# ScalarE evictions, early masks and a split FFN input in a one-core decoder step: what the change does to the time

## The reference: what is computed

```python
h = rms_norm(x, norm_mix_g); z = h @ w_in          # 512 q | 256 kv | 64 k_rope | 1024 u | 1024 v
q = rms_norm(z_q) @ w_q_up                         # 8 heads x (128 + 64 rope)
kv_c = rms_norm(z_kv); k_pe = rope(z_pe)           # latent attention
u = gelu(z_u); v = rms_norm(gelu(z_v))
cm = u * (tril(w_spatial) @ v + b)                 # in chunks of 128 positions
x += concat(rms_norm(attn), rms_norm(cm)) @ w_out
x += memory_attend(rms_norm(x)) @ w_mem_o          # 4 heads of 128, 256 memory tokens
x += square(relu(rms_norm(x) @ w_ffn_up)) @ w_ffn_down     # 8192 wide
```

## Time and profile before

| what | value |
|---|---|
| time, median of 3 runs | 2558.09 us (2555.03 to 2559.18) |
| time of the profiled execution | 2557.49 us |
| its span, first to last instruction | 2555.6 us |
| PE busy | 2417.3 us (95%) |
| DVE, ACT, POOL busy | 895.9, 630.6, 957.3 us (35%, 25%, 37%) |
| mean granted TensorE clock | 0.979 |

### The profile page before, as it was taken

One profiled execution on the slowest core, in us unless ns is written; L12 is line 12 of the kernel. 1 busy time (PEld: TensorE's weight loads), 2 busy tenths in 40 slices (PEclk: granted clock), 3 DMA queues, 4 the chain that ended last, 5 costly groups with the idle time before them and its releaser, 6 DMA issues.

```text
span 2555.6 us, 47459 instructions
## 1 busy us (share of the span) xinstructions
PE 2417.3 (95%) x18906; PEld 2353.2 (92%) x18906; DVE 895.9 (35%) x1257; ACT 630.6 (25%) x888; POOL 957.3 (37%) x412
## 2 busy tenths in 40 slices
PE   7999868688999989999999999999999999999996
PEld 7999858556899878999999999999999999999996
DVE  6200297576533567211211211211211311311366
ACT  5211352254211433211211211211211211211210
POOL 3433352232344323443433434334343343433442
PEclk9999989799999999999999999999999999999998
DMA  6665574375422242222222222222222222222222
GB/s 257 191 187 182 179 245 134 140 299 212 153 88 84 79 170 74 86 87 90 82 90 87 85 90 82 90 87 86 90 82 90 87 86 90 82 90 87 85 90 86
DMA packets 101733, 304.37 MB, mean 119 GB/s; under 512 B 12369, under 2 KB 45170, under 8 KB 96562
## 3 DMA queue, kind: packets, MB, share of 16 engines
q1 hardware_dynamic: 98784, 291.01, 32.9%
q10 hardware_dynamic: 2898, 12.66, 1.3%
HBM read 297.30 MB, written 44.08 MB: 134 GB/s over the span
## 4 chain that ended last, share of the span: by engine, by line
PE 66%; issue 18%; POOL 8%; DVE 7%; ACT 0%; POOLq 0%; DVEq 0%; ACTq 0%
PE psum L1295 63%; POOL hl L387 8%; DVE square L1148 1%; PE psum L1484 1%; DVE square_sum L1150 1%; DVE head_max L1064 1%; PE psum L1446 0%; DVE x L1145 0%; DVE x L1284 0%; DVE probs_t L1103 0%; DVE square L863 0%; DVE probs L1085 0%; DVE head_bias L1066 0%; DVE psum L1059 0%; DVE rstd_x L818 0%
## 5 line engine op out<-in xcount | busy, mean ns | idle before, releaser
L387 POOL TENSOR_TENSOR hl<-raw,hl 128x1024 fp32r<-128x1024 f32 x376 | 917.2, 2440 | 1470.9 <-ACT hl L769 926.2
L1295 PE MATMUL psum<-xg,hl 128*128 128x272 f32 x10272 | 1306.0, 289 | 28.7 <-DVE xg L813 16.7
L1295 PEld LDWEIGHTS psum<-xg,hl 128*128 128x128 f32 x10272 | 1301.4, 189 | 32.3 <-POOL hl L387 16.2
L1295 PE MATMUL psum<-ffn_hidden,hl 128*128 128x272 f32 x6144 | 772.7, 288 | 0.0
L1295 PEld LDWEIGHTS psum<-ffn_hidden,hl 128*128 128x128 f32 x6144 | 771.9, 188 | 0.0
L769 ACT CAST hl<-raw 128x1024 fp32r<-128x1024 f32 x254 | 267.2, 1052 | 1222.8 <-PE psum L1295 1222.8
L1272 DVE TENSOR_TENSOR x<-x,psum 128x544 f32 x112 | 80.8, 721 | 567.2 <-PE psum L1295 567.2
L1257 DVE SCALAR_TENSOR_TENSOR square<-psum,rstd_x 128x544 f32<-128x544 f32 x64 | 46.4, 725 | 496.7 <-PE psum L1295 496.7
L1261 DVE TENSOR_SCALAR ffn_hidden<-square 128x544 f32 x64 | 132.1, 2064 | 60.7 <-ACT square L778 60.7
L448 ACT CAST hl<-raw 128x1024 fp32r<-128x1024 f32 x64 | 67.3, 1051 | 317.7 <-PE psum L1295 317.6
L441 ACT CAST hl<-raw 128x1024 fp32r<-128x1024 f32 x58 | 60.5, 1046 | 183.2 <-PE psum L1295 124.2
(11 more groups left out here) (231 smaller groups left out, 1137.9 us busy)
## 6 DMA issues: line engine op xcount, KB each, us to landing
raw<-in_w_stream SPq DMA_DIRECT2D x376, 512.0 KB, 3.2
page_cols_gathered<-in_pool_t SPq DMA_DIRECT2D x128, 160.0 KB, 2.9
page_cols<-page_cols_gathered SPq DMA_DIRECT2D x16, 1280.0 KB, 7.1
page_rows_gathered<-in_pool_n SPq DMA_DIRECT2D x128, 128.0 KB, 2.9
page_rows<-page_rows_gathered SPq DMA_DIRECT2D x16, 1024.0 KB, 6.2
x<-in_x_t SPq DMA_DIRECT2D x8, 544.0 KB, 9.2
out<-x SPq DMA_DIRECT2D x8, 544.0 KB, 2.7
cache_k_sb<-in_mem_k_t SPq DMA_DIRECT2D x2, 2048.0 KB, 9.7
```

The costliest lines, as they stand in the source:

```text
L387: nc.gpsimd.tensor_tensor(HL[s % 2][:, 1, :, :], RAW[:, s % 4, :, :], HL[s % 2][:, 0, :, :].bitcast(F32), ALU.subtract).then_inc(w_lo, 1)
L1295: last = mm(PSUM[:, s + half, 0:HALF], HL[slot][:, wp, blk, :], src[:, xp, k, HALF * half:HALF * (half + 1)], start=start and n == 0, stop ...
```

## The change

It has five parts.

1. **Region moved.** TB goes up from 72224 to 72288 bytes, and the memory output's operand `OMH` from TB to TB + 121344.
2. **Masks early.** The 16 small multiplications that mask the spatial weights go from DVE's program just ahead of the memory values' eviction to ahead of the evictions of the input projection.
3. **Evictions on ACT.** Every second eviction of the v transposes, and all evictions of q_up and KV, go from DVE to ACT, between the `hi` of the units. DVE then has the four ropes in one piece, the sample group's rope copies, head 0's rope operands and the eight scalings of the mix result.
4. **Head 0's splits early.** ACT's three casts for head 0 stand behind the first half of KV, and POOL's three subtractions ahead of `lo(72)`; the DMA of `w_uv_sb` goes behind `hi(73)`.
5. **FFN input in MEMO.** Per tile DVE adds to x and then makes the lo part of the tile before; ACT makes the hi part and the square (two buffers); POOL adds the squares up. PE's sum of squares goes from ahead of FFN tile 0 to behind it.

The core of the diff:

```diff
-        TB = at_end[0]
+        TB = (at_end[0] + 31) // 128 * 128 + 96
...
-        OMH = place("mem_out_split", [P, 2, MH, TOK], F32R, TB)
+        OMH = place("mem_out_split", [P, 2, MH, TOK], F32R, TB + 121344)
...
             stage_qk_lo(0)
             stage_v_lo(0)
+            for n in range(U_OUT, U_OUT + 2):
+                lo(n, n + 1)
...
+            def add_square(k):
+
+                pool.wait_ge(x3_sq, k + 1)
+                if k == 0:
+                    last = nc.gpsimd.tensor_copy(ACC[:, :], TMP[0][:, :])
+                else:
+                    pool.wait_ge(x3_add, k)
+                    last = nc.gpsimd.tensor_tensor(ACC[:, :], ACC[:, :], TMP[k % 2][:, :], ALU.add)
+                last.then_inc(x3_add if k < KD - 1 else sum_ok, 1)
+
+            for i in range(8):
+                add_square(2 * i)
+                lo(U_MEMO + 2 + i, U_MEMO + 2 + i + 1)
+                add_square(2 * i + 1)
...
             hi(62)
             hi(63)
+            for n in range(1, 8, 2):
+                act.wait_ge(tr, n + 1)
+                nc.scalar.copy(VT[:, n // 2, 512:1024], PSUM[:, 4 + n % 4, :]).then_inc(tr_out_a, 1)
...
+            q_out(0)
+            act.wait_ge(mix_out, 9)
+            for k in range(4):
+                square("c", k, Z[:, Z_U + k, :])
+            hi(64)
+            q_out(1)
+            for k in range(4, 8):
+                square("c", k, Z[:, Z_U + k, :])
+            q_out(2)
+            hi(65)
+            q_out(3)
+            sqrt("c", RX, 6, 1024, TOK, [(kv_n, 2)])
+            for m in range(2, 6):
+                q_out(2 * m)
+                hi(64 + m)
+                q_out(2 * m + 1)
...
-                    act.wait_ge(t_out, G_KV + 16)
+                    act.wait_ge(t_out, G_KV + 8)
...
-            for j in range(2, 12):
-                q_out(j)
-                if j == 5:
-                    invert("c", RX)
-                if j in (6, 7, 9, 10):
...
+            invert("c", RX)
+            for r in range(4):
+                dve.wait_ge(t_out, G_QUP + r + 1)
+                if r:
+                    dve.wait_ge(q_ready, r)
+                rope(Q[:, 8 + r, :]).then_inc(q_ready, 1)
...
+            def x3_tile(k):
+                act.wait_ge(t_out, G_MEMO + k + 1)
+                nc.scalar.activation(XG[:, 0, k, :], X[:, k, :], ACT.Copy,
+                                     scale=G[:, GAINS["x3"] + k:GAINS["x3"] + k + 1]).then_inc(xg_hi, 1)
+                if k > 1:
+                    act.wait_ge(x3_add, k - 1)
+                nc.scalar.activation(TMP[k % 2][:, :], X[:, k, :], ACT.Square).then_inc(x3_sq, 1)
+
+            for i in range(8):
+                x3_tile(2 * i)
+                hi(U_MEMO + 2 + i)
+                x3_tile(2 * i + 1)
             sqrt("x3", RX, 6, D, TOK, [(t_out, G_MEMQ + 4)])
...
+            for k in range(KD):
+                if k % 2:
+                    dve.wait_ge(w_used, U_MEMO + k // 2 + 1)
+                else:
+                    dve.wait_ge(half_used, 7 + k // 2)
+                tt(two(X[:, k, :]), two(X[:, k, :]), banks(G_MEMO + k), ALU.add).then_inc(t_out, 1)
+                if k:
+                    x3_lo(k - 1)
+            x3_lo(KD - 1)
             invert("x3", RX)
...
+            ffn_up_tile(0, 0, 0)
+            sum_squares("x3", 6)
+            ffn_up_tile(0, 0, 1)
```

More of the change, by code:

```diff
@@ L388, in lo @@
                                         HL[s % 2][:, 0, :, :].bitcast(F32), ALU.subtract).then_inc(w_lo, 1)
-            with pool.Fori(0, U_OUT // 4) as i:
+            with pool.Fori(0, U_KV // 4) as i:
                 for s in range(4):
                     lo(s, i * 4 + (s + 1))
-            for n in range(U_OUT, U_OUT + 2):
+            for n in range(U_KV, U_OUT):
                 lo(n, n + 1)
@@ L603, in stage_v_hi @@
                 nc.scalar.copy(VH[:, 0, :, :], VV[:, :, 128 * h:128 * h + 128]).then_inc(v_hi, 1)
+            act.wait_ge(st_mk, 32)
+            q_out(0)
[14 more added lines that the diff above has]
+                q_out(2 * m + 1)
+            act.wait_ge(st_out, 48)
+            for h in range(4):
+                k_out(h, G_KV + h)
+            hi(70)
+            for kb in range(4):
+                v_out(kb, 0, G_KV + 4 + kb)
+            hi(71)
             stage_qk_hi(0)
             stage_v_hi(0)
+            for h in range(4, 8):
+                k_out(h, G_KV + 4 + h)
+            hi(72)
+            for kb in range(4):
+                v_out(kb, 1, G_KV + 12 + kb)
+            hi(73)
+            act.wait_ge(qabs_out, 2)
+            act.dma_start(WUV[:, :, :], w_uv_p).then_inc(ld_uv, 16)
             act.wait_ge(c_n, 8)
@@ L846, in _ @@
                     z_out(4)
+            dve.wait_ge(ld_c, 16)
+            dve.wait_ge(ld_sp, 48)
+            for g in range(8):
+                tt(WT[:, g, :], WT[:, g, :], C[:, C_TRIL:C_TRIL + 128], ALU.mult)
+                last = tt(W4[:, g, :], W4[:, g, :], C[0:NS, C_BLOCK:C_BLOCK + NS], ALU.mult)
+            last.then_inc(mask_ok, 1)
             with dve.Fori(0, 9) as i:
@@ L1008, in _ @@
             step(last)
-            dve.wait_ge(t_out, G_KV + 16)
             def stage_rope(h):
@@ L1031, in _ @@
             stage_rope(0)
+            for k in range(8):
+                g = GAINS["c"] + k
+                stt(Z[:, Z_U + k, :], Z[:, Z_U + k, :], G[:, g:g + 1], RX[:, :], ALU.mult, ALU.mult).then_inc(c_n, 1)
+            dve.wait_ge(t_out, G_KV)
             nc.vector.memset(QR[:, :, :], 0.0)
@@ L1407, in _ @@
             pe.wait_ge(mask_ok, 1)
-            pe.wait_ge(tr_out, 11)
+            pe.wait_ge(tr_out, 6)
+            pe.wait_ge(tr_out_a, 5)
             for g in range(8):
@@ L1735, in _ @@
                         last.then_inc(w_used, 1)
+            ffn_up_tile(0, 0, 0)
+            sum_squares("x3", 6)
+            ffn_up_tile(0, 0, 1)
+            with pe.Fori(1, CHUNK_TILES // 2) as p:
+                for t in range(2):
+                    ffn_up_tile(0, p, t)
+            ffn_down(0)
+            with pe.Fori(1, FFN_CHUNKS) as c:
+                with pe.Fori(0, CHUNK_TILES // 2) as p:
+                    for t in range(2):
+                        ffn_up_tile(c, p, t)
+                ffn_down(c)
             sum_squares("x4", 6)
```

145 lines of the change are left out of this document (56 added, 89 removed).

## The result

The changed kernel takes **2503.06 us** (median of 4 runs, 2499.65 to 2504.43) against 2556.91 in the same comparison, a ratio of 0.9788 (95% interval 0.9777 to 0.9800). The profiled execution's span is 2501.4 us, 54.2 shorter.

What follows compares the result with a forecast made beforehand. PE was taken as the bound, busy 2417.3 of 2555.6 us. Terms -1.1 - 6.4 - 8.0 - 10.3 - 1.9 - 1.4 = -29.1 from 2557.49 gave 2528.4 us, range 2521 to 2542.

Steps and rivals of the forecast that it cites:

- The region: Moving the region by 64 bytes modulo 128 only swaps the two halves' starts, 32 and 96: no effect.
- My rival on the region: Moved region slows the matmuls' reading; 1.7 ns more each loses the whole gain, 3 ns gives 2580 us; chance 0.04.
- The mix: Mix starts earlier through early masks and shared copies, limited by ACT's half behind `hi(63)`: -1.1 us, bounds 0 and -2.8.
- the masks themselves cost nothing: Masks at their new place are free, since DVE has idle time between the input projection's evictions.
- q_up: In q_up, waits of 1.25 and 2.83 us and further losses go: -6.4 us, bounds -4.1 and -8.2.
- KV: In KV, waits of 1.57 and 5.05 us and 2.2 lost beside them go, 0.8 is added: -8.0 us.
- q_abs to the scores: From KV's end to the first scores, 15.8 us becomes 5.5, head 0's parts being ready early: -10.3 us.
- DVE's chain: DVE's ropes, then copies and eight scalings, end by about 458; head 0 begins at 466.
- Head 0: Up to half of 4.2 us at half clock comes back once the wait of 10.95 goes: -1.9 us, bounds 0 and -2.1.
- MEMO: MEMO and the FFN's start: -1.4 us in all, including +1.5 for lost pace, bounds 0 and 3.6.
- The contention: In MEMO, DVE's two-tensor operations don't run beside POOL's: a pair of tiles takes 6.5 us, 0.45 over PE's pace.
- The stop at tile 1: PE stops ahead of FFN tile 1, as unit 122's cast follows ACT's root: 4.6 us, plus 1.7 for the clock.

Runs made afterwards that it cites:

- e9: Changed kernel with the weights' two slots 64 bytes higher and the region's base at 72352: 2504.50 us, ratio 0.9792 to the kernel before.
- e10: Changed kernel with the weights' two slots 64 bytes higher and the region's base at 72416: 2520.32 us, ratio 0.9860 to the kernel before.
- e1: Kernel before with only the region's base 64 bytes higher and the memory output's operand at its new place: 2540.43 us against 2557.86.
- e2: Changed kernel with the region's old base, the memory output's operand staying at TB + 121344: 2521.68 us, ratio 0.9863 to the kernel before.
- e3: Kernel before with only the early masks, evictions on ACT and head 0's early splits, old region: 2526.04 us, ratio 0.9885.
- e4: Kernel before with only the FFN part (input in MEMO, later sum of squares, memory output's operand moved), old region: 2554.50 us, ratio 0.9989.
- e7: Changed kernel with the 16 maskings of the spatial weights back at their old place on DVE: 2511.73 us, ratio 0.9816 to the kernel before.
- e8: Changed kernel with PE's q_abs moved between the two halves of KV: 2500.65 us, ratio 0.9781 to the kernel before.
- e6: Changed kernel with ACT's casts of units 122 and 123 ahead of the square root of x3: 2496.29 us, ratio 0.9763 to the kernel before.

## Why the prediction was wrong, step by step

- **The region, the step that failed most.** "Both halves of a tile are 1088 bytes long, so that one started at 32 and the other at 96 of 128, and afterwards the other way round. In PE's rows both halves are issued at equal distance: nothing." Equal distance was no sign that the place costs nothing: in the trace of before the mean distance behind the two halves differs by 0.3 ns, but single ones go from 122.5 to 129.2, in a pattern that repeats every 12 matmuls. And I looked at the moving operand alone. e9 and e10 show that its place counts against that of the weights, which stayed where they were. The term is 17 us by e1 and 19.0 by the rate. My rival on the region had the place and the leverage right (1.7 ns each makes up 29 us), but I gave it the other sign only. With a term of -19, 2528.4 would have been 2509. The 6 that are left come chiefly from the mix (2.7 beyond its term and the rate) and from the clock between head 1 and MEMO (2.9), both below.
- **The mix, -1.1 forecast.** "But ACT's half stands behind `hi(63)`, which waits for its DMA and ends at 380.03". That landing was taken for fixed. ACT's timeline of the kernel after:

```profile
375.30 1.05 ACT L467 CAST hl<-raw 128x1024 fp32r<-128x1024 f32 x1 [2.39 <-DMA raw<-in_w_stream]
```

  In e1, e2, e3, e4 and e7 it began at 373.89, 377.38, 375.95, 375.63 and 373.92: the 378.99 of the earlier trace rows was the latest of all. And "the masks themselves cost nothing" looked at the place that they go to, not at the one that they leave: there e7 makes them worth 6.25 us at the mix. In the profile of before PE began its transposes later (375.49) and so waited less for the same maskings, but the wait was there, and it is not among those that the prediction counts:

```profile
380.45 3.49 PE L1391 MATMUL psum<-consts_sb,z 128*128 128x128 f32 x16 [3.05 <-DVE v_rows L925]
```

- **q_up, KV, q_abs to the scores:** -6.1, -8.5 and -11.1 for -6.4, -8.0 and -10.3. The releasers told the truth, and the order of ACT's work held. DVE's chain ended at 456.84 for the 458 forecast, and the scores waited 0.52 for its copy of q_abs.
- **Head 0, -1.9 forecast, -0.5 measured.** That half clock "can come back when the wait is gone" is wrong. The clock was at 0.50 from 459.0 to 465.8 after a wait of 0.52 only, and e8 shows that it follows q_abs. The rows of before had it too: the half clock begins at 479.20, while q_abs runs until 476.54 + 4.59 = 481.13, ahead of the wait of 10.95.
- **MEMO.** The +1.5 of lost pace was not there (e4). The contention was: a lo part of DVE takes up to 1.99 us beside POOL (others 0.78), POOL's two adds 3.19 where I had 2.70, and POOL falls behind, one lo every 6.17 us (937.50 to 943.67) against PE's 5.97. But that is 0.2, not 0.45, and in the last pairs only: in the first, one lo comes every 5.97 (901.13 to 907.10) with POOL idle for 0.33. Adding DVE's whole lo parts to POOL's time was the step that failed here. By the estimate from the Trainium skill, GPSIMD Engine Reference, section 4.1 (Engine selection), it would have been 6.7 a pair; an add here is about 2.2 of DVE's 0.72 where DVE gets in between, so the page's twofold is nearer than the 1.77 that I used, and yet the sum by it is farther off. (The 1.77 sets 512 columns on POOL against 544 on DVE; at equal width 1.35 to 0.72 is 1.88.)
- **The stop at tile 1** was forecast at 4.6 and is 4.25, with half clock behind it, and e6 takes both away.
- **Head 1 to MEMO, -5.0 where nothing was forecast.** The rate explains 2.1 (some 1,920 matmuls). The rest is the clock, which the forecast took as unchanged there: the granted clock is 0.50 for 27.3 us of this stretch before and for 17.1 after, and 10.2 us at half clock can cost up to 5.1. The other traces bear it out. With all of the change but the region (e2) it is 27.3 again and the stretch takes 420.42, as before; with the front alone (e3), at the old rate, it is 17.1 and 417.62; in e7, at the new rate, 27.3 and 418.73. So these 2.9 us are not shown to be a gain of any of the five parts. Why one kernel has the 17.1 and another the 27.3 no run shows.

## What to carry to other kernels

A matmul's price is a measured number for one memory map. When an edit moves an operand of the engine that bounds the kernel, price it by what a nanosecond on each matmul would make of the time, with both signs, and try the places beside each other: 64 bytes gave a third of this change's gain. A moved instruction is to be priced where it leaves as well as where it goes, and a wait for a DMA is no fixed point in time. And where a sum or a root moves behind a tile, look at what stands behind its consumer in that engine's program: two casts ahead of a root were worth 6.8 us.

## What was not expected of the hardware

- At a granted clock of 1.00 in both, a 272-column matmul in a dense stream took 124.44, 125.28, 125.56 or 126.11 ns, depending on the places of weights and moving operand to each other to a multiple of 128 bytes, and on the order of the halves. At one place (64) the distance changed within an execution, after stops. The Trainium skill, TensorE: Matmul & The Clock Gate, section "Step-by-step: what each phase is for", says that PE has two independent read ports, so that loading the next weights takes nothing from the running matmul's reading. By that sentence alone the weights' place would not count. Here it does, by 1%: base 72352 gives 0.1255 us with the weights at their old place and 0.1244 with the weights 64 bytes higher (e9). What couples the two is not shown by any run.
- q_abs, 32 matmuls of 32 columns in 3.9 to 5.0 us without a wait over 0.52, was followed by 6.8 us at a granted clock of 0.50 in the kernel after and in e8 alike (in e2, e7, e9 and at 72352 by 3.4 at first). The kernel's second stream of this shape (L1618 in the kernel after, from 592.12 on) has the clock at 0.50 from 595.6 to 602.4, and every kernel here has that in or right behind this stream for 6.8 us or more; but waits of 0.86 and 2.32 stand ahead of it and behind it, so that this place alone would not tell.
